# Down projections with 7 and 8 of 22 squares as seven products, and some lows completed by DMA from HBM

## What is computed

```python
def conv_ffn(h, w_up, conv_w, conv_b, w_down):      # w_up: 2048 x 11264, w_down: 5632 x 2048
    u = h @ w_up
    ...                                             # causal depthwise convolution of width 3, plus conv_b
    gate, val = jnp.split(u, 2, axis=-1)
    return (jax.nn.silu(gate) * val) @ w_down

def reference(x, ...):
    for i in range(DEPTH):
        ...
        h = h + conv_ffn(rmsnorm(h, ln_ffn[i]), f_w_up[i], f_conv_w[i], f_conv_b[i], f_w_down[i])
```

## Time and profile before

| | |
|---|---|
| median of 3 runs | 2487.63 us (2487.46 to 2488.08) |
| profiled execution, its time | 2487.73 us |
| profiled execution, its span | 2485.9 us |
| PE busy in the span | 2477.3 us, 11403 matmuls |
| DVE busy | 2162.0 us |
| ACT busy | 1472.0 us |
| down stage of layer 0, about 882 to 1120 us | PE 238.0, DVE 225.2, ACT 142.2 us busy |

### The profile page before, as it was taken

The page is one execution under the profiler, slowest core; times in us unless marked ns, Lnnn a source line. Parts: engine busy times, 40 slices in busy tenths (PEclk is TensorE's granted clock), DMA queues, the critical chain, the costliest instruction groups (busy, mean ns, idle before and its releaser), DMA issues.

```text
span 2485.9 us, 29114 instructions
## 1 busy us (share of the span) xinstructions
PE 2477.3 (100%) x11403; PEld 2061.0 (83%) x11403; DVE 2162.0 (87%) x2389; ACT 1472.0 (59%) x1436; POOL 44.3 (2%) x54
## 2 busy tenths in 40 slices
PE   9999999999999999999999999999999999999999
PEld 8888788888888888888888888888888888888887
DVE  7888867999999999998778878876699999999998
ACT  6555645766667666556545545544576676756654
POOL 1000000000000000000000000000000000000000
PEclk9999999999999999999999999999999999999999
DMA  8555554767676656577555666654476776755754
GB/s 284 195 187 170 169 186 147 228 202 248 191 251 205 208 187 215 178 238 201 158 156 170 195 198 187 189 169 155 139 249 203 232 217 204 233 185 199 244 172 159
DMA packets 359401, 491.24 MB, mean 198 GB/s; under 512 B 20005, under 2 KB 200437, under 8 KB 356832
## 3 DMA queue, kind: packets, MB, share of 16 engines
q1 hardware_dynamic: 355024, 465.64, 57.1%
q0 software_dynamic: 4000, 23.63, 4.4%
q10 hardware_dynamic: 240, 0.10, 0.0%
HBM read 468.31 MB, written 3.68 MB: 190 GB/s over the span
## 4 chain that ended last, share of the span: by engine, by line
PE 93%; DVE 4%; ACT 1%; DMA 1%; issue 1%; ACTq 0%; SPq 0%
PE psum L2073 47%; PE psum L2077 24%; PE psum L1923 5%; PE psum L1914 5%; PE psum L1915 5%; PE psum L2176 2%; PE psum L2303 1%; DVE w_lo L1143 1%; PE psum L1872 0%; DVE w_lo L1151 0%; PE psum L2267 0%; PE psum L2301 0%; PE psum L2275 0%; ACT w_hi L684 0%; DMA w_raw<-in_f_w_up 0%
## 5 line engine op out<-in xcount | busy, mean ns | idle before, releaser
L2073 PE MATMUL psum<-w_hi,xT 128*128 128x512 f32 x4456 | 1115.0, 391 | 0.0
L2073 PEld LDWEIGHTS psum<-w_hi,xT 128*128 128x128 f32 x4456 | 833.3, 188 | 171.5 <-issue 0.2
L671 ACT ACTIVATE w_hi<-w_raw 128x2048 fp32r<-128x2048 f32 (+1 forms) x350 | 631.3, 1810 | 390.6 <-PE psum L2077 258.3
L1143 DVE TENSOR_TENSOR w_lo<-w_raw,w_hi 128x2048 fp32r<-128x2048 f32 (+1 forms) x332 | 704.9, 2145 | 55.3 <-ACT w_hi L671 54.7
L2077 PE MATMUL psum<-w_lo,xT 128*128 128x512 f32 x2228 | 583.9, 389 | 1.1 <-DVE w_lo L1151 0.9
L2077 PEld LDWEIGHTS psum<-w_lo,xT 128*128 128x128 f32 x2228 | 417.8, 188 | 89.6 <-DVE w_lo L1151 2.2
L1151 DVE TENSOR_TENSOR w_lo<-w_raw,w_hi 128x2048 fp32r<-128x2048 f32 (+1 forms) x174 | 375.8, 2176 | 49.8 <-ACT w_hi L684 49.4
L684 ACT ACTIVATE w_hi<-w_raw 128x2048 fp32r<-128x2048 f32 (+1 forms) x174 | 315.7, 1827 | 154.2 <-PE psum L2077 68.1
L2073 PE MATMUL psum<-w_hi,mixT 128*128 128x512 f32 x992 | 265.3, 389 | 0.0
L1914 PE MATMUL psum<-w_hi,xT 128*128 128x512 f32 x624 | 245.1, 393 | 1.0 <-DVE phase L1296 1.0
L1915 PE MATMUL psum<-w_hi,xT 128*128 128x512 f32 x624 | 243.1, 390 | 0.0
(11 more groups left out here) (203 smaller groups left out, 1795.1 us busy)
## 6 DMA issues: line engine op xcount, KB each, us to landing
w_raw<-in_f_w_up SPq DMA_DIRECT2D x352, 512.0 KB, 5.1
w_raw<-in_f_w_down SPq DMA_DIRECT2D x176, 512.0 KB, 5.2
w_raw<-in_b_w_qkv SPq DMA_DIRECT2D x192, 256.0 KB, 3.8
w_raw<-in_a_w_qkv SPq DMA_DIRECT2D x132, 256.0 KB, 5.1
w_raw<-in_b_w_qkv SPq DMA_DIRECT2D x256, 128.0 KB, 2.7
w_lo<-w_raw POOLq DMA_DIRECT2D x18, 1024.0 KB, 7.1
w_raw<-in_a_w_o SPq DMA_DIRECT2D x16, 1024.0 KB, 5.2
w_raw<-in_b_w_qkv SPq DMA_DIRECT2D x32, 512.0 KB, 6.1
```

The lines of the kernel that those rows point to most:

```text
L671: nc.scalar.activation(w_hi[:, slot, cols], w_raw[:, slot, cols], ACT.Copy).then_inc(hi_ready, 1)
L1143: nc.vector.tensor_tensor(w_lo[:, slot, cols], w_raw[:, slot, cols], w_hi[:, slot, cols], ALU.subtract).then_inc(lo_ready, 1)
L2073: pe.matmul(o, x[:, h, P * m:P * (m + 1)], hi, start=start and h == 0, stop=False)
```

## The change

It does four things.

1. The lists of the two passes become 5 plain squares with groups 2, 3, 2, 2, 2, 2, 3 (seven fast squares) and 3 plain with groups 2, 3, 2, 2, 2, 2, 2, 3 (eight).
2. In both passes the plain square right behind every second "one" gets its low by transfer: three per pass in the first, four in the second, 14 in both layers.
3. The adding transfer reads the weights from HBM instead of `w_raw`, as two transfers of 512 KB, in the up stages too. SP and DVE then need to wait only for the high of such a chunk before the raw slot is written again (`raw_read`).
4. For such a chunk ACT writes the negated weights first and the high second.

```diff
-DOWN_BY_DMA = ()
+DOWN_GROUPS = ((5, (2, 3, 2, 2, 2, 2, 3)), (3, (2, 3, 2, 2, 2, 2, 2, 3)))
...
-DOWN_ENTRIES = [(what, p, j) for p, form in enumerate(((6, (2, 2, 3, 3, 2, 3)), (3, (3, 2, 2, 3, 3, 2, 3)))) for what, j in down_pass(*form)]
+DOWN_ENTRIES = [(what, p, j) for p, form in enumerate(DOWN_GROUPS) for what, j in down_pass(*form)]
+DOWN_BY_DMA = tuple(e + 1 for p in range(HALVES) for i, e in enumerate(
+    e for e, (what, q, j) in enumerate(DOWN_ENTRIES) if (what, q) == ("one", p)) if i % 2 == 1)
...
             if by_dma(c):
                 n = DMA_LOWS.index(c)
-                engine.wait_ge(lo_added[n % 2], 16 * (n // 2 + 1))
+                engine.wait_ge(lo_added[n % 2], 32 * (n // 2 + 1))
             else:
                 at_least(engine, lo_ready, lows(c))
+
+        def raw_read(engine, c):
+
+            if by_dma(c):
+                engine.wait_ge(hi_ready, c + 1)
+            else:
+                at_least(engine, lo_ready, lows(c))
...
             def free_slot(c):
 
-                lo_made(sp, c - SLOTS)
+                raw_read(sp, c - SLOTS)
...
                         pool.wait_ge(lo_negated, n + 1)
-                        pool.dma_start(w_lo[:, c % SLOTS, :], w_raw[:, c % SLOTS, :],
-                                       accum_op=ALU.add).then_inc(lo_added[n % 2], 16)
+                        for tiles, cols in zip((slice(1, 3), slice(0, 4, 3)), weights):
+                            pool.dma_start(tiles_of(w_lo, c % SLOTS)[:, tiles, :], cols,
+                                           accum_op=ALU.add).then_inc(lo_added[n % 2], 16)
...
-                nc.scalar.activation(w_hi[:, slot, cols], w_raw[:, slot, cols], ACT.Copy).then_inc(hi_ready, 1)
                 if by_dma(c):
                     nc.scalar.activation(w_lo[:, slot, :], w_raw[:, slot, :], ACT.Copy, scale=-1.0).then_inc(lo_negated, 1)
+                nc.scalar.activation(w_hi[:, slot, cols], w_raw[:, slot, cols], ACT.Copy).then_inc(hi_ready, 1)
...
             def add_weights(c, to):
 
                 dve.wait_ge(w_in[c % SLOTS], landed(c))
-                lo_made(dve, to - SLOTS)
+                raw_read(dve, to - SLOTS)
                 sum_tiles(c, to)
```

More of the change, by code:

```diff
@@ L461, in lo_made, with weights_up, weights_down @@
                 n = DMA_LOWS.index(c)
[L462 removed]
+                engine.wait_ge(lo_added[n % 2], 32 * (n // 2 + 1))
             else:
                 at_least(engine, lo_ready, lows(c))
+        def raw_read(engine, c):
[3 more added lines that the diff above has]
+                at_least(engine, lo_ready, lows(c))
+        def weights_up(layer, t, j):
+            rows = f_w_up[layer, 256 * j:256 * (j + 1), :].rearrange("(k p) c -> p k c", p=P)
+            return [rows[:, :, at:at + F][:, :, bass.ts(t, 512)] for at in (0, F)]
+        def weights_down(layer, p, j):
+            rows = f_w_down[layer, 256 * j:256 * (j + 1), 1024 * p:1024 * (p + 1)].rearrange("(k p) c -> p k c", p=P)
+            return [rows[:, :, at:at + 512] for at in (0, 512)]
         def chunk_used(engine, c):
@@ L550, in load_up_block @@
                     free_slot(c + e)
-                    rows = f_w_up[layer, 256 * j:256 * (j + 1), :].rearrange("(k p) c -> p k c", p=P)
                     dst = tiles_of(w_raw, slot)
-                    sp.dma_start(dst[:, 1:3, :], rows[:, :, 0:F][:, :, bass.ts(t, 512)]).then_inc(w_in[slot], 16)
-                    sp.dma_start(dst[:, 0::3, :], rows[:, :, F:2 * F][:, :, bass.ts(t, 512)]).then_inc(w_in[slot], 16)
+                    for tiles, cols in zip((slice(1, 3), slice(0, 4, 3)), weights_up(layer, t, j)):
+                        sp.dma_start(dst[:, tiles, :], cols).then_inc(w_in[slot], 16)
             def load_ffn(layer):
@@ L565, in load_ffn @@
                     free_slot(c + e)
-                    rows = f_w_down[layer, 256 * j:256 * (j + 1), 1024 * p:1024 * (p + 1)].rearrange(
-                        "(k p) c -> p k c", p=P)
                     dst = tiles_of(w_raw, slot)
-                    sp.dma_start(dst[:, 1:3, :], rows[:, :, 0:512]).then_inc(w_in[slot], 16)
-                    sp.dma_start(dst[:, 0::3, :], rows[:, :, 512:1024]).then_inc(w_in[slot], 16)
+                    for tiles, cols in zip((slice(1, 3), slice(0, 4, 3)), weights_down(layer, p, j)):
+                        sp.dma_start(dst[:, tiles, :], cols).then_inc(w_in[slot], 16)
             for p in range(A_PAIRS):
@@ L625, in add_lows @@
                     if UP0[layer] <= c < DN0[layer] + DOWN:
+                        if up_entry(c) is not None:
+                            t = max(t for t in range(UP_BLOCKS) if UP_FIRST[t] <= up_entry(c))
+                            weights = weights_up(layer, t, UP_ENTRIES[t][up_entry(c) - UP_FIRST[t]][1])
+                        else:
+                            weights = weights_down(layer, *DOWN_ENTRIES[down_entry(c)][1:])
                         pool.wait_ge(lo_negated, n + 1)
-                        pool.dma_start(w_lo[:, c % SLOTS, :], w_raw[:, c % SLOTS, :],
-                                       accum_op=ALU.add).then_inc(lo_added[n % 2], 16)
+                        for tiles, cols in zip((slice(1, 3), slice(0, 4, 3)), weights):
+                            pool.dma_start(tiles_of(w_lo, c % SLOTS)[:, tiles, :], cols,
+                                           accum_op=ALU.add).then_inc(lo_added[n % 2], 16)
             pool.wait_ge(a_row_in, 16)
```

2 lines of the change are left out of this document (1 added, 1 removed).

## The result

The changed kernel takes 2547.36 us (2546.72 to 2549.34) against 2487.55 us for the kernel before on the same chip. The ratio is 1.0242 with an interval of 1.0229 to 1.0255: 59.8 us slower, where I had forecast 2.7 us less.

What follows compares the result with a forecast made beforehand. The prediction took PE to bound the kernel (busy 2477.3 of 2485.9 us), so 2487.7 - 2.7 for PE, with no cost from DVE, ACT or adds, gave 2485.0 us; the 8-in-10 range was 2484 to 2500 us.

Steps and rivals of the forecast that it cites:

- PE's term: Down stages: four more fast squares, each 21 matmuls for 24, save 0.68 us each, 2.7 us in all.
- DVE's sum: Down stages: fast squares add 23.7 us, 14 lows leaving save 30.8; DVE has 7 us less, no cost.
- ACT's term: Down stages: 14 more chunk passes and four fast squares add some 34 us to ACT; no cost by itself.
- The adds in the up stages: Adds now read HBM, 18 MB more; PE leaves 20 us before the lows, so no cost.
- The adds in the down stage: Lows behind every second "one": add lands about 8.0 us after first issue; nothing to 4.9 us each, nothing likeliest.
- My upper bound: Down-stage adds sharing engines with loads: landing 2.75 us later beside one load, 5.5 beside two; up to 4.9 us each.
- the low end: Down-stage adds: each costs nothing, as it lands in about 8.0 us, within the slack.
- larger slack: Down-stage adds with ACT free: 11.6 us left less 8.0 to landing, 3.7 us; otherwise 0.6 us.
- Rival 1: Lows behind every second "one": adds share engines with loads and PE waits; 14 x 1.1 = 15 us, 2500 us; chance 0.28.
- Rival 2: Down-stage sums: DVE waits for the load the add delays; 4 x 1.5 = 6 us, 2491 us; chance 0.20.
- the likeliest case: Whole kernel: PE saves 2.7 us and down-stage adds cost nothing; 2485.0 us, chance 0.50.

Runs made afterwards that it cites:

- small adds: The change with each down-stage add cut to 32 of 512 columns per tile, lows left unfinished: 2496.61 us; with groups of two starting at even squares, 2487.07 us.
- quarter adds: Lists with groups of two at even squares; one tile of four of each following low added by transfer, DVE makes the other three: 2512.04 us, 1.0102.
- aligned lists: The change with lists of seven and eight fast squares whose groups of two start at even squares; with complete adds from HBM 2530.28 us, 1.0172.
- e2_adds_only: Old lists of squares, with the low behind every second "one" made by an add from HBM, 12 in both layers: 2514.41 us, 1.0114.

## Why the prediction was wrong

- **PE's term: right.** 12 matmuls less; 1.36 us less in the one stage that had no new wait.
- **DVE's sum: right in work, not in place.** DVE is 6.2 us less busy (7 foretold), and a full group takes 11.45 us (11.5 foretold). "Cost at DVE: none, covered by at least 2 us, if loads come as before" failed at its condition: half loads took up to 13.0 us, where they take 5.2 at the median before. I also counted the activation block as 1.14 us of work and never asked when its slot comes free and when PE wants it. That was 9.5 us by itself with small adds, 7.5 without adds.
- **ACT's term: right.** 32.7 us more busy, 34 foretold.
- **The adds in the up stages: right**, no cost (ratio 1.0002).
- **The adds in the down stage: the step that failed.** "I take nothing for the likeliest". The sum took a landing 8.0 us after the first issue and so no wait; the landing was at 13.3 us at the median (12.7 to 14.2), and PE waited 25.4 us in 12 of 14 places. My upper bound was nearly right: 8.0 us and 2.75 more for each load beside it gives 10.8 and 13.5, and between an add's issue and its landing SP's queue moved 1.6 to 2.5 MB, about two loads. Of my reasons for the low end, "SP's load is issued some 3 us into the add" was true (2.3 and 2.7 us for its halves) and worthless: another load was issued 0.7 us into the add, and the add had moved nothing by then. "Most adds have the larger slack" was true as well: in 11 of 14 places PE wanted the low 11.1 us or more after the issue, in the other three after 9.4 to 10.0. A landing at 13.3 us is too late for the larger slack too. The bounds on one add were from nothing to 4.9 us; 3.1 was measured, lost clock included.
- **The rule of the Trainium skill** that all issuers' transfers interleave on the same 16 engines ("DMA: Bandwidth & Descriptors", "Issuing engines are not separate DMA queues") describes the stretch from 912 to 920, where POOL's queue had 70.8% of the engines and SP's 37.8%; I should have given it the larger chance. From 909 to 912 the trace shows less than that for the add: SP's queue alone. The other rule of the Trainium skill, that POOL can't write descriptors while DVE holds the port in its two-port mode ("SBUF — State Buffer", "SBUF: two separate sides"), is not seen: beside the same DVE work the one-piece issues took 0.84 to 0.90 us, and the quarter adds landed after some 4 us without a load beside them and after some 6 with one, DVE busy throughout in both.
- **Rival 1 (2500): right in kind, too small.** It let an add cost 1.1 us on average, for it counted one load beside it. By its own working two loads give 5.5 - 3.7 = 1.8 us with the larger slack, and PE's waits for adds are 25.4 / 14 = 1.8 us each. Two more things were missing. The add and the loads all finish late, so DVE and ACT are late too and the next wait is no shorter; and the matmuls behind a wait were slower, below.
- **Rival 2 (2491): its first half happened.** DVE's wait for loads is 36.7 us in all, 17.7 of them in layer 0, near the 20 that I had named. But PE did not wait for a low of DVE; it waited for DVE's block of activations, where the lists had left no room. That its price of 6 us is near the 8.2 of the copied bytes may be chance.

I had both rivals as alternatives. Both come of the add sharing the engines with loads, and the likeliest case needed both to be absent.

## What to carry to other kernels

An added transfer that shares full DMA engines with loads gets no right of way by being issued first: here its first bytes moved 3.1 to 5.0 us after the issue in the down stages. So add up the engine time of all that is in flight in the stretch and compare the sum (13.6 us in the stretch above, where the landing took 13.1) with the slack, for the new transfer and for the loads that it delays. If the sum is larger than the slack, that is the forecast and not the rival. And when the order of squares is changed, check every buffer's release against its next use: the activations' as well as the weights'.

## What was not expected of the hardware

**TensorE after a wait.** In the changed kernel the matmuls behind the wait of 3.41 us ran at a granted clock of 0.66 over the stretch, part of it at 2.4 GHz and part, as the second line shows, at 1.2 GHz:

```profile
934.00:939.00 5.00, 4.81 (x14) 3.84 (x15) 4.93 (x6) 3.00 (x3) 0.00 (x0) 0.66 0.26 97
936.00:938.00 2.00, 2.00 (x6) 1.58 (x5) 1.97 (x2) 0.04 (x1) 0.00 (x0) 0.50 0.02 8
...
977.00:979.00 2.00, 1.66 (x7) 1.40 (x8) 1.32 (x2) 1.03 (x1) 0.00 (x0) 1.00 1.05 389
```

The last line is the stretch behind another wait of 3.39 us in the same kernel, at full clock. With aligned lists eight such lows take 1.98 us without a wait. Behind waits they took:

```profile
953.20 2.76 PE L2097 MATMUL psum<-w_lo,xT 128*128 128x512 f32 x8 [3.78 <-DMA w_lo<-in_f_w_down]
977.77 3.33 PE L2097 MATMUL psum<-w_lo,xT 128*128 128x512 f32 x8 [2.27 <-DMA w_lo<-in_f_w_down]
...
1065.48 2.11 PE L2097 MATMUL psum<-w_lo,xT 128*128 128x512 f32 x8 [2.19 <-DMA w_lo<-in_f_w_down]
1090.29 3.23 PE L2097 MATMUL psum<-w_lo,xT 128*128 128x512 f32 x8 [4.12 <-DMA w_lo<-in_f_w_down]
```

The length of the wait ahead does not tell which: the clock also fell behind one of 1.83 us. What it costs in sum is plain for these two kernels: 21.1 us beside 40.6 us of waits in the changed kernel, 16.8 beside 30.7 with aligned lists and complete adds (PE busy 2492.4 against 2475.6 with small adds, profiled spans 2532.7 against 2485.2). There a wait of PE cost about half as much again as its length. It need not: with the old lists and 12 adds (`e2_adds_only`) PE waited 23.1 us in the down stages, up to 2.5 us at a time, and the granted clock was 1.00 over both stages. What decides it stays open.

**Issues on POOL.** A transfer of 512 KB with rows of 2 KB in HBM took POOL 1.19 to 1.72 us to issue, one of 1 MB with rows of 8 KB 0.85, and one of 256 KB with rows of 2 KB 0.85 too. Here that did not matter.
